# One plain fp32 product in place of three fp32r products with leading parts and remainders

## The reference, cut to what matters

```
q_x, k_x, v_x, u_x, b_x, c_x, ga_x, gc_x = split(einsum('btd,df->btf', hx, w_in))
...
merged = sigmoid(g_attn) * (o_attn @ w_proj_attn) + sigmoid(g_conv) * (y_conv @ w_proj_conv)
x = x + g1 * (merged @ w_out)
...
xe = h[idx]                                   # 64 tokens for each of 16 experts
ye = (silu(xe @ w_gate) * (xe @ w_up)) @ w_down * gate
...
x = x + (gelu(conv(x @ w_up[:, :FF])) * (x @ w_up[:, FF:])) @ w_down    # FF = 2816
```

## Time and profile before

| | |
|---|---|
| median of 3 runs | 1966.28 us (1966.18 to 1968.85) |
| time of the profiled execution | 1966.39 us |
| its span | 1964.6 us |
| mean granted TensorE clock | 0.975 |
| PE busy | 1847.9 us (94%) |
| DVE busy | 984.2 us (50%) |
| ACT busy | 654.6 us (33%) |
| DMA mean | 181 GB/s over the span |

### The profile page before, as it was taken

How to read it: one execution, slowest core, us unless ns; L and a number is a source line. 1 busy time by engine, 2 the same in 40 slices (tenths; PEclk the granted TensorE clock), 3 DMA queues, 4 the chain that set the end, 5 groups by cost and what they waited for, 6 DMA issues and landing times.

```text
span 1964.6 us, 22766 instructions
## 1 busy us (share of the span) xinstructions
PE 1847.9 (94%) x9403; PEld 1337.4 (68%) x9403; DVE 984.2 (50%) x1620; ACT 654.6 (33%) x1126; POOL 85.4 (4%) x70
## 2 busy tenths in 40 slices
PE   6989999999999699999999899999899899999998
PEld 4877777778878434343443278887777688888886
DVE  4888877752553412222222153637484656535643
ACT  4455544442242302020110052424545332222233
POOL 0200000000000000000000000003030200000000
PEclk8999999999999799999999999999899999999999
DMA  9333333252333399999999943262111422233221
GB/s 322 125 106 99 108 107 97 87 193 86 114 142 159 129 394 421 422 421 422 420 421 421 415 155 102 70 199 84 43 65 43 151 85 86 89 116 107 73 89 43
DMA packets 174521, 355.10 MB, mean 181 GB/s; under 512 B 7154, under 2 KB 144466, under 8 KB 149074
## 3 DMA queue, kind: packets, MB, share of 16 engines
q1 hardware_dynamic: 170672, 338.85, 46.9%
q10 hardware_dynamic: 3458, 14.50, 2.0%
q0 software_dynamic: 288, 0.30, 0.1%
HBM read 345.53 MB, written 8.39 MB: 180 GB/s over the span
## 4 chain that ended last, share of the span: by engine, by line
PE 77%; DVE 10%; ACT 5%; DMA 4%; issue 2%; POOL 1%; SPq 0%; ACTq 0%; DVEq 0%
PE ps L491 75%; PE ps L494 2%; DMA rx<-in_w_exp_down 1%; DMA rx<-in_w_exp_gate 1%; DVE small L2134 1%; ACT M L1245 1%; POOL X L2803 1%; DVE wsp0l L1889 1%; DMA md<-in_w_mod 1%; DVE wsq1l L1889 1%; DVE X L1898 1%; ACT KR L1245 1%; POOL tb L2803 1%; DVE wsp1l L1889 0%; DVE tb L1889 0%
## 5 line engine op out<-in xcount | busy, mean ns | idle before, releaser
L491 PE MATMUL ps<-H,wsq1h 128*128 128x512 f32 x640 | 200.3, 394 | 4.7 <-DVE wsq1l L1889 2.7
L491 PE MATMUL ps<-H,wsq0h 128*128 128x512 f32 x608 | 191.0, 396 | 0.2 <-DVE wsq0l L1889 0.2
L491 PE MATMUL ps<-rx,XE 128*64 128x512 f32 x752 | 176.5, 600 | 2.9 <-DMA rx<-in_w_exp_up 2.2
L491 PE MATMUL ps<-H,wsp1h 128*128 128x512 f32 x544 | 172.8, 399 | 1.4 <-DVE wsp1l L1889 1.4
L491 PEld LDWEIGHTS ps<-H,wsq1h 128*128 128x128 f32 x640 | 120.2, 190 | 30.5 <-issue 6.1
L491 PEld LDWEIGHTS ps<-H,wsq0h 128*128 128x128 f32 x608 | 114.5, 190 | 25.4 <-issue 2.3
L491 PE MATMUL ps<-H,wsq1l 128*128 128x512 f32 x320 | 125.3, 392 | 0.0
L491 PE MATMUL ps<-H,wsp0h 128*128 128x512 f32 x368 | 121.0, 407 | 2.1 <-ACT H L1245 2.1
L1889 DVE TENSOR_TENSOR wsq1l<-ring,wsq1h 128x1024 fp32r<-128x1024 f32 (+2 forms) x72 | 82.9, 1191 | 77.9 <-ACT wsq1h L1245 77.9
L491 PE MATMUL ps<-H,wsq0l 128*128 128x512 f32 x304 | 119.0, 392 | 0.0
L491 PEld LDWEIGHTS ps<-H,wsp1h 128*128 128x128 f32 x544 | 100.0, 190 | 22.0 <-issue 3.5
(11 more groups left out here) (378 smaller groups left out, 3465.8 us busy)
## 6 DMA issues: line engine op xcount, KB each, us to landing
rx<-in_w_exp_gate SPq DMA_DIRECT2D x49, 1024.0 KB, 16.9
rx<-in_w_exp_down SPq DMA_DIRECT2D x46, 1024.0 KB, 20.7
rx<-in_w_exp_up SPq DMA_DIRECT2D x45, 1024.0 KB, 19.3
ring<-in_w_in SPq DMA_DIRECT2D x37, 1024.0 KB, 5.4
ring<-in_w_up SPq DMA_DIRECT2D x20, 1024.0 KB, 5.1
ring<-in_w_exp_up SPq DMA_DIRECT2D x19, 1024.0 KB, 20.6
ring<-in_w_mod SPq DMA_DIRECT2D x18, 1024.0 KB, 6.9
ring<-in_w_exp_down SPq DMA_DIRECT2D x18, 1024.0 KB, 19.2
```

The source lines that it names most:

```text
L491: return pe.e.matmul(o, l, r, start=start, stop=stop, skip_group_check=True)
```

## The change

All three-matmul units become one matmul on the unsplit slab and the unsplit activation, both fp32. The split buffers, `hi`, `lo_half`, `ahead`, the `left...` functions, `rope_hi`, `rope_lo`, `query_hi`, `query_lo` and the four transfers are gone, and PE waits for a slab's transfer directly. SP reuses a ring slot when PE has used the slab, no longer when DVE has split it. `gather` and `combine` take one fp32 matmul in place of two in fp32r. The scores take q and k of 64 rows, head 0 in the upper and head 1 in the lower half of the array's rows, with the two latent products next to each other. The memory set free gives a twelfth `rx` slot; eight expert slabs are now issued among the slabs of `gc pc ga pa`, one behind each `proj`, and four more may follow before `wo` ends. The scale 0.125 moves to the copy of the keys, or to the exponential. The second attention's rope result goes from POOL straight to q2 and k2. Half of each pair's result Y is scaled by DVE, half by ACT.

```
-                wh, wl = hi_lo(s)
...
-                        pe.wait_ge(S["v_lo"], (s.key, half_of(s, k)))
-                        mm(o, wh[:, k, c], hh[:, kk, 0:N], kk == 0, False)
-                        mm(o, wh[:, k, c], hl[:, kk, 0:N], False, False)
-                        i = mm(o, wl[:, k, c], hh[:, kk, 0:N], False, kk == tot - 1)
+                        i = mm(o, w[:, k, m * P:(m + 1) * P], h[:, kk, 0:N], kk == 0, kk == tot - 1)
...
+        def weights(s):
+            pe.wait_ge(S[s.slot], s.key)
+            return s.raw
...
-                mm(bank(b), Yh[:, c * P:(c + 1) * P], GT[pr % 2], True, False)
-                mm(bank(b), Yl[:, c * P:(c + 1) * P], GT[pr % 2], False, True).then_inc(*S["pe_combine"].tick((pr, c)))
+                mm(bank(b), Y[:, c * P:(c + 1) * P], GT[pr % 2], True, True).then_inc(*S["pe_combine"].tick((pr, c)))
...
                 for i in range(4):
-                    for n, part in enumerate(gathered(q, c)):
-                        t = mm(bank(b, 0, 256), part[:, i, :], Gn[:, i, :], i == 0 and n == 0, i == 3 and n == 1)
+                    t = mm(bank(b, 0, 256), htv[:, i, c * P:(c + 1) * P], Gn[:, i, :], i == 0, i == 3)
...
+            def ctx(i):
+                return mm(bank(3, 256 * i, 256 * i + 256), q[heads[i], :], KCd[heads[i], g, :], True, True)
+            ctx(0).then_inc(*S["pe_score"].tick((g, n, 0)))
             for i in range(2):
+                mm(ps[:, lat[i]:lat[i] + W], q[heads[i], :], Kd[heads[i], g, lo:hi], True, False)
...
+            pe.wait_ge(S["pe_score"], (g, n, 0))
+            ctx(1).then_inc(*S["pe_score"].tick((g, n, 1)))
...
+    for gate, proj, w, c0 in (("gc", "pc", a["w_proj_conv"][0], 5632), ("ga", "pa", a["w_proj_attn"][0], 4608)):
         for n in range(4):
+            piece((gate, n), w_in, 0, 8, c0 + 256 * n)
+            piece((proj, n), w, 0, 8, 256 * n)
+            expert_slab()
...
     def over(s):
-        if s.turn is not None:
-            return "v_lo", (s.key, 1)
+        if s.key in final:
+            return "pe_group", final[s.key]
```

More of the change, by code:

```diff
@@ L90, in __init__ @@
         self.raw = place[:, 0:nk * cols].rearrange("p (k n) -> p k n", n=cols)
-        self.flat = place[:, 0:nk * cols]
-        self.before, self.after, self.turn = before, after, None
-        self.halves, self.last = None, None
+        self.before, self.after = before, after
 def r128(v):
@@ L337, in rows, with slab @@
         return w[k0 * P:(k0 + nk) * P, c0:c0 + cols].rearrange("(k p) n -> p k n", p=P)
-    def slab(key, sources, nk, cols, slot=None, place=None, after=(), split=True):
+    def slab(key, sources, nk, cols, slot=None, place=None, after=()):
         if slot is None:
@@ L345, in slab, with piece @@
         last_in[slot] = s
[L346 to L355, removed]
+    def piece(key, w, k0, nk, c0, cols=256, slot=None, place=None):
+        slab(key, [(0, cols, rows(w, k0, nk, c0, cols))], nk, cols, slot, place)
     early = [4, 0, 5, 1, 6, 2, 7, 3]
@@ new lines, in emit, with expert_slabs @@
+    past_md = [("pe_mod", (early[7], "raw"))]
+    turns = [(f"rx{i}", rx[i], past_md if i < 3 else ()) for i in range(8)]
+    def expert_slabs():
+        for pr in range(8):
+            for e in (2 * pr, 2 * pr + 1):
+                for which, w in (("g", a["w_exp_gate"]), ("u", a["w_exp_up"])):
+                    for k in range(4):
+                        yield e, which, w, k
+            for k in range(4):
+                for e in (2 * pr, 2 * pr + 1):
+                    yield e, "d", a["w_exp_down"], k
@@ new lines, in emit, with expert_slab @@
+    experts = enumerate(expert_slabs())
+    def expert_slab():
+        j, (e, which, w, k) = next(experts)
+        slot, place, after = turns[j % 16 if j < 188 else j - 188]
+        pairs = w[0][e][2 * k * P:(2 * k + 2) * P, :].rearrange("(p k) n -> p k n", k=2)
+        slab((which, e, k), [(0, 1024, pairs)], 2, 1024, slot, place, after)
+    for gate, proj, w, c0 in (("gc", "pc", a["w_proj_conv"][0], 5632), ("ga", "pa", a["w_proj_attn"][0], 4608)):
+        for n in range(4):
+            piece((gate, n), w_in, 0, 8, c0 + 256 * n)
+            piece((proj, n), w, 0, 8, 256 * n)
+            expert_slab()
@@ L387, in emit @@
     for n in range(4):
         piece(("wo", n), a["w_out"][0], 0, 8, 256 * n)
[L390 to L394, removed]
-    places = [(6, past_v), (4, past_a), (5, past_a), (0, past_kr), (1, past_kr), (2, past_m), (3, past_m)]
-    first = len(slabs)
@@ L397, in emit @@
-    turns = [(f"rx{i}", rx[i], after) for i, after in places]
-    turns += [(f"ring{(len(in_ring) + i) % 4}", ring[(len(in_ring) + i) % 4], ()) for i in range(4)]
-    turns += [(f"rx{i}", rx[i], past_h) for i in range(7, 11)]
-    def expert_slab(e, which, w, k):
-        slot, place, after = turns[(len(slabs) - first) % len(turns)]
-        pairs = w[0][e][2 * k * P:(2 * k + 2) * P, :].rearrange("(p k) n -> p k n", k=2)
-        slab((which, e, k), [(0, 1024, pairs)], 2, 1024, slot, place, after, split=False)
@@ L450, in emit @@
             piece(("dn", half, n, 1), wdn, 11 * half + 6, 5, 256 * n)
-    def after_split(s):
-        return splits[s.turn + 1] if s.turn + 1 < len(splits) else None
     where, final = {}, {}
-    def hi_lo(s):
-        n = s.nk * s.cols
-        return [h[:, 0:n].rearrange("p (k n) -> p k n", n=s.cols) for h in s.halves]
-    first_second = slabs[("u2", 0)].turn
-    def split_free(s):
-        if s.turn in (first_second, first_second + 1):
-            return "pe_down", ("d", 15, 3)
-        return "pe_group", final.get(s.last.key)
-    def half_of(s, k):
-        return 0 if 2 * (k + 1) <= s.nk else 1
     early_units, units = 8, 4 * 7 + 8 * 12
@@ L566, in wide, with lin_n @@
                 yield k
-        def lin_n(key, hh, hl, toks, frees):
-            for h in range(2):
-                s = slabs[key + (h,)]
-                wh, wl = hi_lo(s)
+        def lin_n(key, h, toks, frees):
+            for half in range(2):
+                s = slabs[key + (half,)]
+                w = weights(s)
                 for n, cols in enumerate(toks):
-                    if h == 0:
+                    if half == 0:
                         take((key, n), frees(n))
@@ L802, in tensor @@
             scored = (g, n)
-            for _ in range(paced(it, 2)):
-                next(more)
+            for _ in behind:
+                pass
         for _ in more:
@@ L1047, in tensor @@
         for n in (1, 2):
[L1048 removed]
+            lin([("u2", n)], H2v, T, lambda m: [("v_take", (("u2", n), m))], behind=rows if n == 1 else None)
         b = take("ws", [("v_gmlp", "wsT")])
@@ L1130, in beside2 @@
             for key in fills2:
-                yield from steps([key], H2h, H2l, T, lambda m: [("v_take", (key, m))])
+                yield from steps([key], H2v, T, lambda m: [("v_take", (key, m))])
         more = beside2()
@@ L1245, in act @@
             return ac_.e.activation(o, i, f, **kw)
-        def hi(s):
-            if s is None or s.key in split:
-                return
-            split.add(s.key)
-            wh = s.halves[0]
-            n = s.nk * s.cols
-            for h in range(2):
-                c = slice(h * n // 2, (h + 1) * n // 2)
-                ac_.wait_ge(S[s.slot], s.key)
-                if s.turn > 2:
-                    ac_.wait_ge(S[split_free(s)[0]], split_free(s)[1])
-                act(wh[:, c], s.flat[:, c], ACT.Copy).then_inc(*S["a_hi"].tick((s.key, h)))
-        def ahead(key):
-            s = slabs[key]
-            hi(s)
-            if after_split(s) is not slabs["u2", 0]:
-                hi(after_split(s))
         def load(name, key, out_, in_):
@@ L1424, in values @@
                 *S["a_value"].tick((g, n)))
-        for _ in fill(fills[0]):
-            pass
-        hi(slabs["q", 0, 1])
-        query_hi(owed.pop())
-        hi(slabs["conv", 0, 0])
         def beside():
@@ L1442, in scalar @@
             soft(g, n)
+            if it == 0:
+                for _ in range(early_units - 4):
+                    next(more)
             for _ in range(paced(it, 0)):
@@ L1446, in scalar @@
                 values(*turned)
-            for _ in range(paced(it, 1)):
-                next(more)
             turned = scored
@@ L1838, in scalar @@
             for n in range(6):
-                ahead(("up", half, n))
                 for m in range(2 if n < 5 else 1):
@@ L1844, in scalar @@
                         *S["a_gmlp"].tick(("ff", (half, n, m))))
-                ahead(("val", half, n))
-                for m in range(2 if n < 5 else 1):
-                    ac_.wait_ge(S["v_take"], (("val", half, n), m))
-                    ac_.wait_ge(S["pe_group"], final.get(("dn", 0, 3, 1) if half else ("wo2", 3)))
-                    act(hfhv[:, 2 * n + m, :], acv[:, m, :], ACT.Copy).then_inc(*S["a_put"].tick(("hf", half, 2 * n + m)))
             if half:
@@ L1852, in scalar @@
             for n in range(4):
```

(2 more changed lines are left out.)

817 lines of the change are left out of this document (213 added, 604 removed).

## The result

The changed kernel takes 2265.67 us in the median (2264.46 to 2266.81, 3 runs) against 1966.28: 1.151 times the time before, 95% interval 1.1493 to 1.1526. The forecast was 2260, range 2215 to 2320. The profiled execution has a span of 2265.1 us, 300.5 more than before.

What follows compares the result with a forecast made beforehand. The prediction took PE, busy 1847.9 of 1964.6 us, as the bound. Units +287.7, other PE work +66 and relief -59.5 made +294, so 1966.4 + 294 = 2260 us, range 2215 to 2320.

Steps and rivals of the forecast that it cites:

- The price of a unit: All 1616 units on PE: 0.858 us each in place of 0.680, 0.178 dearer, +287.7 us.
- four passes at an fp32r pass's 0.2267: Rival for every unit on PE: 0.907 us each, +79, 2340 us in all; chance 0.05.
- weight loads in the open: Rival: loads no longer overlap, two of 0.19 us a unit, +614, 2875 us; chance 0.02.
- a price of 0.454: Rival "Faster": a full-width fp32 matmul costs two fp32r steps, sum near 1610 us; chance 0.03.
- the loaded stages swallow their share: Rival: net growth in the attentions and expert stage (42 + 6 + 38) vanishes, 2175 us; chance 0.05.
- Splits off PE's path give nothing: ACT and DVE split work gives nothing where PE runs without a gap; its removal gives back only idle time.
- Scores: First attention's 32 blocks: +6 to +24, the top for row halves in turn, taken +10; second attention's: taken +2.
- Gather: Gather in the expert stage: +0.75 us for each of 32 blocks, +24.
- combine: Combine products on PE: 1.06 us in place of 0.66, +0.40 x 64 = +25.6.
- The relief: Idle time and waits given back over the whole kernel: -59.5 us.
- its -25 for the second attention and merge: Waits for k2h and M2, late splits and the lowered clock there given back: -25, bounds -12 and -40.
- The expert stage: Transfers stop being last, so waits there go: -11.5; twelfth slot and earlier slab issue buy nothing more.

Runs made afterwards that it cites:

- experiment 2: Kernel before with one plain fp32 matmul for each three-matmul unit, splits still made but remainders unused: 2210.64 us, 1.1223.
- experiment 7: Changed kernel with head 0's masks between the two heads' latent products, so the row halves can't stream together: 2294.72 us.
- experiment 8: Changed kernel with the second attention's queries and strided keys read as 128 neighbouring tokens in place of every fourth: 2253.20 us.
- Experiment 5: Changed kernel with gather and combine as two one-pass matmuls on the upper halves of the words: 2224.36 us, 1.1288.
- experiment 6: Changed kernel with no expert slab issued before the last product of wo, all twelve rx slots waiting for it: 2267.33 us.
- experiment 3: Changed kernel with each unit but the 96 of v2 and av as three one-pass bf16 matmuls on upper half-words: 1991.84 us, 1.0111.
- experiment 10: Kernel before with six in place of four pieces of the gates' products ahead of the second attention's first scores, fewer behind later blocks: 1954.93 us, 0.9937.

## Why the prediction was right, point by point

The stages can be laid over each other, since PE runs them in the same order. Lengths in us, from the marks named (last `onesrow,acc` product of the first attention, last bias product of the router, first gather, last down product, last copy of `av`, last product with `vr`, second-last row spread, end); the last column is what the forecast's terms give for the same stretch:

| stretch | before | before, fp32 units (2) | after | after - before | forecast |
|---|---|---|---|---|---|
| start and first attention | 411.9 | 438.9 | 460.5 | +48.6 | +42 |
| gates and projections | 174.8 | 220.4 | 220.4 | +45.6 | +45.6 |
| `wo` and router | 84.5 | 94.5 | 93.1 | +8.6 | +11.4 |
| experts | 461.8 | 464.9 | 499.2 | +37.4 | +35 |
| `u2` to `av` | 199.0 | 243.6 | 243.6 | +44.6 | +47 |
| second attention | 189.7 | 201.9 | 208.6 | +18.9 | |
| `bb`, `wo2`, start of `up` | 80.7 | 94.1 | 89.4 | +8.7 | |
| feed-forward | 362.2 | 450.2 | 450.3 | +88.1 | |
| the last three together | 632.6 | 746.2 | 748.3 | +115.7 | +114 |

- **The price of a unit**, 0.858 from two matmuls of the earlier trace rows and a half-width stream, was exact: 45.6 us forecast and measured in the stage that is nothing else. The rival of four passes at an fp32r pass's 0.2267 would have made it 58 us, and fell. The Trainium skill (FP8 and Floating Point Precision, TensorE Precision Notes) says that true fp32 takes four passes; the trace agrees, if each is taken at 0.429 / 2 = 0.2145 (it shows two records and not the passes). The rivals of weight loads in the open and of a price of 0.454 fell by the same row of the timeline. (The prediction's 0.013 for a weight change is 0.012 by its own two numbers, and its upper bounds add to 2327 where the range ends at 2320; neither bears on the outcome.) The rival by which the loaded stages swallow their share fell too: the first attention with the start grew by 48.6 us and the expert stage by 37.4.
- **Splits off PE's path give nothing** where it has no gap: shown in experiment 2, to 0.1 us over the 450 of the feed-forward part. The prediction calls that part one without a gap, and that was misread: the earlier trace rows has 9.6 us idle in it. Of the 9.6 some 8 are left in experiment 2 and in the changed kernel alike, so they are not the splits'.
- **Scores were mis-sized.** I took +10 and +2. A block of W = 384 went from 1.54 to 2.23 us and one of W = 256 from 1.19 to 1.90 (268.53 to 270.43, below), 0.7 x 32 = +22; a block of the second attention from 3.7 at full clock (1410.28 to 1413.96 in the kernel before) to 5.3 (1575.38 to 1580.68), +13.

```profile
268.53 1.13 PE L438 MATMUL ps<-KD,Q 64*128 64x256 f32 x6
269.59 0.28 PE L438 MATMUL ps<-mk 128*128 128x128 bf16 x2
269.80 0.70 PE L438 MATMUL ps<-KD,Q 64*128 64x256 f32 x2
270.43 3.70 PE L438 MATMUL ps<-H,ring 128*128 128x512 f32 x8
```

The term that was mis-sized is the estimate from columns alone: it left out the changes between half and full rows (experiment 7; 0.2 + 0.11 + 0.2 = 0.5 of the 1.90) and the stride of four words (experiment 8). The upper end of +24 in the prediction stood for row halves in turn, which did not happen; that +22 lies under it is luck. Gather was dearer by 0.67 a block in place of 0.75 (975.81 to 977.63, 1.82 us), combine by 0.40 as forecast (971.92 to 972.98, 1.06).
- **The relief was larger than I wrote.** The work added is 288 + 4.5 + 22 + 13 + 26 + 21 = 374 us, the span grew by 300.5: 74 us went, not 59.5. The recorded idle time has 55 of them. The rest is about what the granted clock gave back, by my estimate 24 us at most (what falls on idle time costs nothing): 0.975 over 1964.6 us loses 49 against full clock, 0.989 over 2265.1 loses 25. The forecast has the clock only inside its -25 for the second attention and merge, though it stood at 0.84 in `wo` and the router, 0.94 in the second attention and 0.96 behind it, and is 0.88, 1.00 and 1.00 now. By stage: the start and first attention gave 26 us where I had 21, as twenty microseconds of idle time in the first attention all went (0.8 left) where I had given half. From the second attention to the end it was 34 us in place of 25. So the forecast's two errors, 21 us too little work and 14 too little relief, nearly cancelled; its total is better than its parts, and that is luck.
- **The expert stage** changed its bound as forecast: transfers last before, PE after. Its waits gave back less than I wrote: gather, and the combines of the seven pairs that fall in this stretch, add 44 us of work, the stage grew by 37.4, so 6 to 7 us went and not 11.5. Its +37 beside a forecast of +35 is again two errors, this one and gather's. Experiment 5 brings the old price and the old bound back together; experiment 6 shows that the early slabs bring nothing. Whether the twelfth slot brings anything was not run.

## What to carry to other kernels

Price a change of number format as start-to-start time of the actual record for each unit of work, from whatever stream of that format the trace already holds, even one of two matmuls, and multiply by the count; passes counted on paper are only comparable if each is taken at its own measured step. Work taken from engines off the critical path is worth the idle time of the bound engine and the lowered clock behind it, so first look how much of both there is in each stage, and whether it can be closed directly: here two numbers in the order of the products gave 12 us, while the rewrite that removed the splits cost 300. When a stage's two limits lie within 5% of each other, as transfers and PE in the expert stage, a small addition to one of them is hidden in part (here 44 us of work cost 37), and issuing the other's work earlier loses its worth.

## What the runs showed of the hardware that was not expected

- A plain fp32 product of 64 rows and 128 columns whose two operands both lie four words apart takes 0.76 us to the start of its mask, with neighbours 0.41; its two weight loads take 0.54 and 0.29 us (experiment 8). Which operand costs how much was not run.
- Products in the upper and in the lower 64 rows of the array do stream at the same time: two of 384 columns behind one of 256 take 1.27 us in all, where in turn they would need 0.43 + 0.64 + 0.64 = 1.71 and the change to the masks besides. Going from such products to a full-row one costs 0.2 us, the way back 0.11 (experiment 7).
- A bf16 pass read as every second half-word, with weights of 128 columns, costs the same 0.227 us as an fp32r pass (experiment 3: 174.70 us for 256 units of three), 0.012 more than half a plain fp32 record.
- Idle time on PE cost more than itself: two waits shortened by 5.4 us in all made the stretch 11.9 us shorter, as the granted clock went from 0.94 to 0.99 (experiment 10).
